# Sixteen merge-gate tiles computed as eight pairs of seven block products

## The reference

```python
h = rmsnorm(x, norm_mix_pre)
parts = split(h @ w_in, SPLIT_SIZES)          # ... last part: N_BRANCHES * D_MODEL gate logits
o_a = nsa_mixer(...)    # compressed, selected and sliding-window attention, 8 heads
o_b = gla_mixer(...)    # chunked gated linear attention, 4 heads
o_c = moba_mixer(...)   # causal attention over blocks, 8 heads of 64
merged = sum(sigmoid(gate_b) * (o_b @ w_branch_b) for the three branches)
x = x + rmsnorm(merged @ w_out, norm_mix_post)
x = x + rmsnorm(swiglu_ffn(rmsnorm(x, norm_ffn_pre)), norm_ffn_post)
```

## Time and profile before

| | us |
|---|---|
| median of 3 runs | 911.66 (911.61 to 911.70) |
| profiled execution, its own time | 911.39 |
| its span, first to last instruction | 909.7 |
| TensorE busy | 902.2 (99%) |
| VectorE busy | 632.3 (70%) |
| ScalarE busy | 494.6 (54%) |
| GpSimd busy | 176.1 (19%) |

### The profile page before, as it was taken

The page is one execution under the profiler, slowest core; times in us unless marked ns, Lnnn a source line. Parts: engine busy times, 40 slices in busy tenths (PEclk is TensorE's granted clock), DMA queues, the critical chain, the costliest instruction groups (busy, mean ns, idle before and its releaser), DMA issues.

```text
span 909.7 us, 14373 instructions
## 1 busy us (share of the span) xinstructions
PE 902.2 (99%) x5236; PEld 795.3 (87%) x5236; DVE 632.3 (70%) x1173; ACT 494.6 (54%) x928; POOL 176.1 (19%) x192
## 2 busy tenths in 40 slices
PE   9999999999999999999999999999999999999997
PEld 8888888888888888888888888989999999988886
DVE  5998656372555555656657748867888888779776
ACT  6744245343556665767664436345555655556562
POOL 3000254334133333435410001100001000000000
PEclk9999999999999999999999999999999999999999
DMA  9323626222323233274326943477777862334662
GB/s 346 127 74 89 200 93 214 88 93 93 101 85 96 91 101 103 84 266 127 122 91 253 329 149 116 151 154 229 188 245 204 227 173 101 108 159 161 210 205 96
DMA packets 43154, 139.62 MB, mean 153 GB/s; under 512 B 4884, under 2 KB 7508, under 8 KB 42332
## 3 DMA queue, kind: packets, MB, share of 16 engines
q1 hardware_dynamic: 37260, 116.16, 36.9%
q0 software_dynamic: 4992, 18.88, 9.0%
q10 hardware_dynamic: 832, 3.67, 1.4%
HBM read 124.83 MB, written 32.54 MB: 173 GB/s over the span
## 4 chain that ended last, share of the span: by engine, by line
PE 96%; DVE 2%; DMA 1%; ACT 1%; issue 0%; SPq 0%; DVEq 0%; ACTq 0%
PE bank L2237 27%; PE bank L2239 27%; PE bank L2238 27%; PE bank L833 3%; PE bank L825 2%; PE bank L850 2%; PE bank L848 2%; PE bank L824 2%; PE bank L2302 1%; PE bank L2256 1%; DMA xT<-x_features 1%; DVE pcs L685 1%; PE bank L2436 0%; PE bank L2492 0%; PE bank L2352 0%; PE bank L2423 0%
## 5 line engine op out<-in xcount | busy, mean ns | idle before, releaser
L1137 ACT ACTIVATE w_hi<-w_raw 128x1024 fp32r<-128x1024 f32 (+1 forms) x84 | 88.4, 1054 | 124.5 <-PE bank L2239 121.0
L2237 PE MATMUL bank<-h_hi,w_lo 128*128 128x512 f32 x352 | 140.5, 399 | 0.0
L2238 PE MATMUL bank<-h_lo,w_hi 128*128 128x512 f32 x352 | 137.5, 391 | 0.0
L2239 PE MATMUL bank<-h_hi,w_hi 128*128 128x512 f32 x352 | 137.4, 390 | 0.0
L1547 DVE TENSOR_TENSOR w_lo<-w_raw,w_hi 128x1024 fp32r<-128x1024 f32 (+2 forms) x63 | 77.0, 1223 | 40.5 <-ACT w_hi L1137 40.2
L712 DVE CUSTOM_DVE_ANT_0 sc<-bank,fullb 128x512 f32<-128x512 f32 (+1 forms) x96 | 47.0, 490 | 77.8 <-PE bank L825 76.0
L609 ACT ACTIVATE sc<-sc,ast 128x512 f32<-128x512 f32 (+1 forms) x96 | 53.8, 561 | 72.8 <-DVE ast L712 72.7
L1051 POOL TENSOR_TENSOR sc<-sc,ast 128x512 f32<-128x512 f32 (+1 forms) x96 | 66.3, 723 | 130.6 <-DVE ast L734 97.7
L2238 PE MATMUL bank<-tx_lo,op_hi 128*128 128x256 f32 x288 | 81.5, 283 | 0.0
L2239 PE MATMUL bank<-tx_hi,op_hi 128*128 128x256 f32 x288 | 81.5, 283 | 0.0
L2237 PE MATMUL bank<-tx_hi,op_lo 128*128 128x256 f32 x288 | 81.5, 283 | 0.0
(11 more groups left out here) (375 smaller groups left out, 2410.7 us busy)
## 6 DMA issues: line engine op xcount, KB each, us to landing
w_raw<-wpack SPq DMA_DIRECT2D x126, 512.0 KB, 3.7
down_sums<-wpack POOLq DMA_DIRECT2D x18, 768.0 KB, 7.0
dn_right<-down_sums SPq DMA_DIRECT2D x12, 768.0 KB, 4.2
dn_right<-wpack SPq DMA_DIRECT2D x9, 768.0 KB, 4.3
gate_logits<-gl_out SPq DMA_DIRECT2D x24, 256.0 KB, 2.2
gl_in<-gate_logits SPq DMA_DIRECT2D x24, 256.0 KB, 5.5
down_sums<-down_sums POOLq DMA_DIRECT2D x6, 768.0 KB, 5.9
near_bias<-near_bias ACTq DMA_DIRECT2D x1, 2880.0 KB, 13.5
```

The costliest lines, as they stand in the source:

```text
L1137: sa.activation(split_weights(c)[0][:, 0:n], raw[:, s, 0:n], ACT.Copy).then_inc(w_hi, 1)
L2237: mm(out, ll, rh, start=start, stop=False, skip_group_check=True)
L2238: mm(out, lh, rl, start=False, stop=False, skip_group_check=True)
L2239: return mm(out, lh, rh, start=False, stop=stop, skip_group_check=True)
```

## The change

Eight gate tiles stay as they are (units 0 to 31). The other sixteen are taken in pairs: two tiles are a 256 x 512 result, with a model dimension of 1024, and the pair is computed as a 2 x 2 block product with seven instead of eight block products (Winograd's form, the same as in the FFN). Each block product is 4 steps of `three` over 256 tokens. A pair takes eight units, with 4, 3, 4, 3, 4, 3, 4, 3 steps in them.

- **Weights.** The blocks b11, b12, b21, b22 are packed in the weight array; the sums t1 to t4 are made in DRAM by GpSimd with 16 copying and adding transfers of 1 MiB, fourteen in the straight stage and two in units 2 and 6 of the attention. A weight piece is now 128 x 512, and there are seven per pair, with splits and fetches at units set by a table.
- **Sums of h.** VectorE forms s1, s2, s4 and s3 of the halves of h in units 6 to 28 and 35, ScalarE their highs in units 13, 17, 23 and 34.
- **Results.** A pair uses two banks. ScalarE copies four intermediate results (256 columns each) and VectorE joins three, all at the head of a unit, for a product that ended in the unit before. Five buffers in SBUF hold the results: three for the left tile in turn, two for the right one. SP stores both tiles in the first two units of the next pair.
- **Room.** The sums and buffers lie where `cks` and `cv` were. So SP stores all MoBA keys and values to DRAM before the attention (2 MiB each), and loads keys, swapped keys and values per head into rings of two.

The diff, cut to what the text speaks of:

```diff
+G_PLAIN = 8
+G_PAIRS = (N_GATES - G_PLAIN) // 2
+GATE_OPS = (("b11", "a11"), ("t1", "s1"), ("t2", "s2"), ("b22", "s4"), ("t3", "s3"), ("b21", "a12"), ("t4", "a22"))
+STEP_FROM = (0, 4, 7, 11, 14, 18, 21, 25, 28)
...
+    at = {C_GATE + k: UNITS_PER_GATE * (k - 2) + 5 for k in range(2, G_PLAIN)}
...
+        at[C_PAIRED + o] = U_PAIRED + UNITS_PER_PAIR * q + (1, 3, 4, 5, 6, 7, 8)[i]
...
+EARLY_SUMS = {5 + 2 * n: divmod(n, 8) for n in range(14)}
+GATE_SUMS_AT = {2: (1, 6), 6: (1, 7)}
...
 # attention_act, at the head of unit u
+                if r == 1 and 0 <= q < G_PAIRS:
...
+                    gate_product(sa, len(GATE_OPS) * q)
+                    sa.activation(gl_left(q)[:, 0:256], pair_bank(q, 0), ACT.Copy).then_inc(gl_copied, 1)
+                elif r == 3 and 0 <= q < G_PAIRS:
...
+                    gate_product(sa, len(GATE_OPS) * q + 1)
+                    sa.activation(gl_right(q)[:, 256:512], pair_bank(q, 1), ACT.Copy).then_inc(gl_copied, 1)
...
 # attention_act, at the end of unit u
+                if u in (13, 17, 23):
...
+                    sa.activation(hs_hi[name][:, :, :], hs[name][:, :, :], ACT.Copy).then_inc(tx_hi, 1)
...
+                for c in HIGH_AT.get(u, ()):
+                    hi(c)
 # attention_dve: sums of h, then at the head of unit u the joins
+                if u == 6:
+                    ve.wait_ge(xT_in[2], 64)
+                    h_whole(h21, first, late)
+                elif u == 8:
+                    h_whole(h_other, second, late)
...
+                if r == 5 and 0 <= q < G_PAIRS:
+                    gate_product(ve, len(GATE_OPS) * q + 3)
+                    ve.wait_ge(gl_copied, G_PLAIN + GATE_COPIES * q + 3)
+                    ve.tensor_tensor(gl_right(q)[:, 0:256], pair_bank(q, 3), gl_right(q)[:, 0:256],
+                                     ALU.subtract).then_inc(joined_out, 1)
...
-                if u % 4 == 2 and 0 <= u // 4 - 1 < N_GATES + 2:
-                    lo(C_GATE + u // 4 + 1)
+                h_sums(u)
+                for c in LOW_AT.get(u, ()):
+                    lo(c)
 # attention_pe
+                elif u < len(UNITS):
+                    q, r = divmod(u - U_PAIRED, UNITS_PER_PAIR)
+                    for step in range(STEP_FROM[r], STEP_FROM[r + 1]):
+                        gate_step(te, three, q, *divmod(step, 4))
...
+        def gate_step(te, three, q, i, k):
...
+                elif i == 1:
+                    te.wait_ge(gl_copied, G_PLAIN + GATE_COPIES * q)
+                elif i < 5:
+                    te.wait_ge(gl_copied, G_PLAIN + GATE_COPIES * q + i - 1)
+                else:
+                    te.wait_ge(joined_out, 3 * q + i - 4)
...
 # SP
+            for t in range(NT):
+                sp.wait_ge(tm_free[t], TM_USE["cv"] + 1)
+            sp.dma_start(cv_dram.rearrange("n p d -> p n d"), cv[:, :, :, :].rearrange("p n t d -> p n (t d)").bitcast(F32)
+                         ).then_inc(xT_in[2], 16)
             single_out(sp, slot_of("ck", 3))
             single_out(sp, slot_of("ck", 2))
-            swap(ckx[:, 0, :], cks[:, 0, :], ck_swap[0])
+            sp.dma_start(ck_dram.rearrange("n p d -> p n d"), cks[:, :, :].bitcast(F32)).then_inc(xT_in[2], 16)
...
                     if n >= 8:
-                        swap(ckx[:, n % 2, :], cks[:, n - 6, :], ck_swap[n % 2])
+                        moba_keys(n + 2)
...
+                n = LAST_OF.get(u - PV_LAG - 1)
+                if n is not None and 8 <= n < N_HEADS - 2:
+                    sp.wait_ge(pv_done, u - PV_LAG)
+                    moba_values(n + 2)
...
+                for c in FETCH_AT.get(u, ()):
+                    if c == C_BR + 3:
+                        sp.wait_ge(gl_stored[1], 16 * (N_GATES // 2))
+                    fetch(c)
 # GpSimd, straight stage, after the low of chunk c + 2
+                if c in EARLY_SUMS:
+                    pool.wait_ge(w_hi, c + 1)
+                    gate_sums(*EARLY_SUMS[c])
```

More of the change, by code:

```diff
@@ L149, with split_at, by_unit, packed_row @@
 assert UNITS_PER_GATE * N_GATES == len(UNITS) and UNITS_PER_GATE == 4
+U_PAIRED, UNITS_PER_PAIR = UNITS_PER_GATE * G_PLAIN, 2 * UNITS_PER_GATE
+STEP_FROM = (0, 4, 7, 11, 14, 18, 21, 25, 28)
+def split_at():
+    at = {C_GATE + k: UNITS_PER_GATE * (k - 2) + 5 for k in range(2, G_PLAIN)}
+    for o in range(4):
+        at[C_PAIRED + o] = U_PAIRED - 3 + (0, 1, 3, 3)[o]
+    for o in range(4, N_GATE_OPS):
+        q, i = divmod(o - 4, len(GATE_OPS))
+        at[C_PAIRED + o] = U_PAIRED + UNITS_PER_PAIR * q + (1, 3, 4, 5, 6, 7, 8)[i]
+    at[C_BR], at[C_BR + 1] = len(UNITS) - 2, len(UNITS)
+    at[C_BR + 2], at[C_BR + 3] = len(UNITS) + 5, len(UNITS) + 9
+    return at
+def by_unit(table):
+    units = {}
+    for c in sorted(table):
+        units.setdefault(table[c], []).append(c)
+    return units
+SPLIT_AT = split_at()
+HIGH_AT = by_unit(SPLIT_AT)
+LOW_AT = by_unit({c: u + 1 for c, u in SPLIT_AT.items()})
+FETCH_AT = by_unit({c: max(len(UNITS) + 2 if c == C_BR + 3 else 3, SPLIT_AT.get(c - RAW_SLOTS, 0) + 1 + (c < C_PAIRED + RAW_SLOTS)) for c in range(C_GATE + RAW_SLOTS, C_BR + RAW_SLOTS)})
+EARLY_SUMS = {5 + 2 * n: divmod(n, 8) for n in range(14)}
+GATE_SUMS_AT = {2: (1, 6), 6: (1, 7)}
+def packed_row(c):
+    return c if c < C_PAIRED else c - PACKED_LESS
 def operand(p, name):
@@ L408, in program, with gate_product, pair_bank, gl_left @@
         block = ctx.enter_context(nc.Block())
+        def gate_product(eng, o):
+            eng.wait_ge(w_used, C_PAIRED + o + 1)
+        def pair_bank(q, i):
+            return bank[6 + (q + (i in (1, 3, 5))) % 2][:, 0:256]
+        def gl_left(q):
+            return gl_first if q == 0 else gl_out if q % 2 else gl_later
+        def gl_right(q):
+            return raw[:, (C_BR + 3) % RAW_SLOTS, 512:CHUNK] if q % 2 else gl_even[:, :]
+        def right_of(name, k):
+            if name in hs:
+                return hs_hi[name][:, k, :], hs_low[name][:, k, :]
+            row = 4 * (name in ("a12", "a22")) + k
+            mine = slice(256, 512) if name in ("s3", "a22") else slice(0, 256)
+            return hh[:, row, mine], hl[:, row, mine]
         def landed(eng, slot, turn):
@@ L806, in branch_part @@
                 last.then_inc(p_full if part == 0 else w_used, 1)
+        def gate_step(te, three, q, i, k):
+            o = len(GATE_OPS) * q + i
+            c = C_PAIRED + o
+            right = GATE_OPS[i][1]
+            if k == 0:
+                te.wait_ge(w_hi, c + 1)
+                lo_split(te, c)
+                if i == 0 and q == 0:
+                    te.wait_ge(gl_copied, G_PLAIN - 1)
+                elif i == 0:
+                    te.wait_ge(joined_out, 3 * q)
+                elif i == 1:
+                    te.wait_ge(gl_copied, G_PLAIN + GATE_COPIES * q)
+                elif i < 5:
+                    te.wait_ge(gl_copied, G_PLAIN + GATE_COPIES * q + i - 1)
+                else:
+                    te.wait_ge(joined_out, 3 * q + i - 4)
+                if q == 0 and 1 <= i <= 4:
+                    te.wait_ge(tx_lo, i)
+            xh, xl = right_of(right, k)
+            high, low = split_weights(c)
+            cols = slice(P * k, P * k + P)
+            last = three(pair_bank(q, i), high[:, cols], low[:, cols], xh, xl,
+                         i in (0, 1, 5) and k == 0, i in (3, 5, 6) and k == 3)
+            if k == 3:
+                last.then_inc(w_used, 1)
         def attention_pe(te, mm, three):
@@ L894, in swap, with moba_keys, moba_values @@
                 sp.dma_start(dst[0:64].bitcast(F32), src[64:128].bitcast(F32)).then_inc(done, 16)
+            def moba_keys(n, swapped=True, own=True):
+                if swapped:
+                    for half in range(2):
+                        rows, other = slice(64 * half, 64 * half + 64), slice(64 - 64 * half, 128 - 64 * half)
+                        sp.dma_start(ckx[rows, n % 2, :].bitcast(F32), ck_dram[n - 8, other, :]).then_inc(ck_swap[n % 2], 16)
+                if own:
+                    sp.dma_start(ckr[:, n % 2, :].bitcast(F32), ck_dram[n - 8, :, :]).then_inc(ck_swap[n % 2], 16)
+            def moba_values(n):
+                sp.dma_start(cvr[:, n % 2, :, :].rearrange("p t d -> p (t d)").bitcast(F32), cv_dram[n - 8, :, :]
+                             ).then_inc(xT_in[n % 2], 16)
             def near_bias(n):
```

242 lines of the change are left out of this document (199 added, 43 removed).

## The result

| | before | after |
|---|---|---|
| median | 911.66 us (5 runs, 911.61 to 912.24) | 916.55 us (5 runs, 915.07 to 917.44) |
| profiled span | 909.7 us | 914.8 us |

What follows compares the result with a forecast made beforehand. TensorE's own work, busy 99% of the span, was taken as the bound. Terms -6.7 + 0.5 + 0.5 + 1.0 = -4.7 us took the profiled 911.39 to 906.7, with 0.27 for the median 907.0; range 902 to 912.5.

Steps and rivals of the forecast that it cites:

- TensorE, -6.7 us: Gate parts of paired tiles: 5.14 us per pass against 5.56, over 16 passes 6.7 us saved; bounds 3.9 to 9.4.
- Rival 4: Gate matmuls: weight load binds, starts over 131 ns; at 150 ns a pair loses 1.5 us, so 924; chance 0.02.
- ScalarE and VectorE within the pairs: Pair passes: neither engine is over capacity, order counts; 0.5 us booked for lost units, bounds 0 to 2.5.
- Rival 1: MoBA passes: ScalarE takes over, its 2.63 us waits per pass all stay, so 920; chance 0.11.
- Sums of h: First 32 units: VectorE's twelve operations of 1.226 us, 14.7 us, fit in 26 us of idle time; booked at nothing.
- The sixth unit: VectorE waits for MoBA keys and values to reach DRAM before the first h sum; 0.5 us, bounds 0 and 2.6.
- The burst: Start of MoBA: queued loads of 5.77 MB make keys for unit 80 late; 1.0 us, bounds 0 and 3.0.
- GpSimd's sums in DRAM: GpSimd issues 16 DRAM sums of 1 MiB, about 9.3 us each; booked at nothing, up to 1.5 us.
- the gain is eaten by stalls: Sixth unit, burst and lags at their bounds (2.6 + 3.0 + 2.5) cancel 6.7 and more: 911 to 913; chance 0.12.

Runs made afterwards that it cites:

- e3: Changed kernel with GLA's 2 MiB load-back in eight pieces at units 73 to 87 and the logit loads at units 89 to 95; 911.11 us.
- e9: e4 with ScalarE's high of `h21` right behind its first right copy at the head of unit 35, the low left in place; 906.93 us.
- e1: Changed kernel with VectorE's eleven operations on h of units 6 to 28 one unit later, ScalarE's highs at units 15, 19, 23; 914.04 us.
- e11: Changed kernel with VectorE's eleven operations on h one unit later, ScalarE's highs left at units 13, 17 and 23; 913.99 us.
- e4: Changed kernel with the edits of e1 and e3, plus the store of a finished gate tile ahead of its unit's fetch; 908.10 us.
- e2: Changed kernel with the twelve h operations and four highs cut to two columns per row, TensorE reading unsummed h; 912.40 us.
- e7: Changed kernel with the 2 MiB load-back issued on ScalarE's queue at the same unit; 915.21 us.
- e8: e4 with ScalarE's high of `h21` at the end of unit 35 and its low at unit 36; 909.32 us.
- e12: Changed kernel with only ScalarE's highs moved, to units 15, 19 and 23, VectorE's h operations left in place; 916.94 us.
- e5: Changed kernel with only the h operations of units 18 and 26 moved, to 19 and 27; 918.43 us.
- e6: Changed kernel with the six h operations of units 8, 12, 16, 20, 24 and 28 one unit later; 915.69 us.

## Why the prediction was wrong

**TensorE, -6.7 us: right.** 42 starts of 120 ns, 5.05 us against the 5.14 forecast. Ten passes gained 4.36 us, 0.44 each; sixteen would give 7.0. Rival 4, the weight load, did not come: the starts lie well below its limit (11.1 us over 84 starts is 132 ns; the prediction has 131).

**ScalarE and VectorE within the pairs, 0.5 us: about right.** The passes from unit 36 to 75 are 8.62 to 8.93 us without a wait of note. In MoBA two passes (76 and 84) stay at 9.28 to 9.3 in e3 and e9, 0.65 us above their neighbours; some 0.2 of it is a wait for a probability low, the rest stays open (VectorE, forecast at 15.0 of 17.4 us, is busy 18.47 of 20 us there, from 436 to 456 us). Rival 1, ScalarE taking over, did not come: undisturbed, it still idles 0.50 + 0.20 + 0.55 + 0.52 = 1.77 us in a pass of 9.3, against the earlier trace rows; I had forecast 0.9.

```profile
435.26 0.62 ACT L737 ACTIVATE sc<-sc,ast 128x384 f32<-128x384 f32 x1 [0.50 <-DVE ast L902]
437.82 0.51 ACT L737 ACTIVATE sc<-sc,ast 128x256 f32<-128x256 f32 x1 [0.20 <-DVE ast L902]
439.65 0.40 ACT L737 ACTIVATE sc<-sc,ast 128x128 f32<-128x128 f32 x1 [0.55 <-DVE ast L902]
441.73 0.72 ACT L737 ACTIVATE sc<-sc,ast 128x512 f32<-128x512 f32 x1 [0.52 <-DVE ast L902]
```

**Sums of h, booked at nothing: the first step that failed, 3.6 us.** The prediction counted idle time (26 us) against work (14.7 us) and let a unit run over into a next one that "has no second large operation". The count was not at fault: it took a MoBA stretch, but from 236 to 312 us, where the sums stand, the kernel before leaves VectorE idle for 32.3 of 76 us, which is more. Three other things were wrong. The 1.226 us came from a row in which VectorE had SBUF to itself, and half of the operations were put right where GpSimd starts its scaling: 1.95 to 2.02 us. The next step of TensorE's chain, the maximum, stands directly behind, so idle time elsewhere in the pass is no cover. And the delay does not stay on VectorE: by way of the exponential it reaches ScalarE's weight high and comes back as VectorE's wait for it (1.14 us). e1 shows the place as the cause, since the same work one unit later costs nothing up to unit 32, and e11 shows VectorE's part of it. The rest is the pass of unit 32, 1.25 us longer than before and 1.64 longer than in e9, and there it is ScalarE: the high of `h21`, which I had booked with the sums, stands ahead of the copy that TensorE waits for, behind another copy that waited 2.63 us for a store. With the high behind the copy the pass falls by 0.9 us (9.67 to 8.74, e4 to e9), of which the next pass takes back 0.4; the 0.4 us of the store ahead of the fetch (10.10 to 9.67, e1 to e4) are within the scatter of this pass.

That slowing was to be had from the Trainium skill before the fact ("GPSIMD Engine Reference", section "Key points"): GpSimd shares its SBUF interfaces with VectorE and contends with VectorE instructions that have two SBUF inputs. The trace agrees, 2.02 against 1.21 us and 3.74 against 2.76. The page gives no price, and by itself the rule would have misled too: e1 has the scaling slow and loses nothing.

**The sixth unit, 0.5 us: right in size.** VectorE waits 0.4 us for the dump of the keys, and unit 12 starts 0.45 us later. With the sum in unit 7 it is gone (e1), and with VectorE's wait but a short operation behind it too (e2); so it takes the wait and the full sum in that place together.

**The burst, 1.0 us with a bound of 3.0: the second step that failed, 5.7 us.** The mechanism was the one named, with place and releaser; the size was not. The prediction had 5.77 MB at 340 GB/s from unit 72, the keys 18.2 us later. They came 22.3 us after it (398.42 to 420.76), 4.1 us later than that. Its count was right: SyncE's list from 398.42 to the keys adds up to 5.5 MiB. But some 7.1 MB moved in that time (317 GB/s over 22.3 us), 1.3 more than counted; by the same list they must be what was still under way at unit 72, such as a fetch issued just before it, and transfers issued behind the keys (values and three weight pieces, 1 MiB, from 411.40 to 415.19 us). At 340 GB/s 1.3 MB is 3.9 us. The remaining 0.2 us is the slow start, 171 GB/s in the stretch from 400 to 402 us, less what the later 365 to 393 GB/s gave back: SyncE issued the load-back only at 404.62, 3.8 us into unit 73, behind a store (402.74) and a fetch (404.19), which by the code wait for a join and for a weight low. TensorE itself came 18.1 us after unit 72 instead of 17.4, so the wait is 4.2 us. To it come 1.6 us at the lower clock, for which the sum had no term at all. That the term would be nothing with another queue is not borne out, as far as e7 goes: with the load-back on a queue of its own 2.8 us of wait stay, and the keys take as long to land, though still behind the logits. Nor do loads in one queue land strictly in the order of their issue: in the changed kernel a weight piece issued at 408.39 landed 10.6 us later, and the two swapped key loads issued behind it, from 409.61 on, took 8.3 and 8.4 us and were there before it.

**GpSimd's sums in DRAM, at nothing: about right.** Twelve take 8.7 us each and four 6.4, against the 9.3 taken. The attention starts 0.38 us later than before in the changed kernel, and from 0.30 earlier to 0.72 later in the experiments (2.15 in the profiled execution of e4). **The rivals.** That the gain is eaten by stalls had 0.12, with a price of 911 to 913, and is what happened; it went past its bounds because both stalls did. That e9 comes out at 906.93, where the prediction had 907.0, is no excuse: it is the time of another order of the same work.

## What to carry to other kernels

Idle time counts only between the two steps that it separates: before adding work to an engine that is 70% busy, look at what stands directly behind it in that queue, and what the neighbours do at that moment. A bound for a burst should start from when the queue really issues, and a wait of TensorE of the length seen here should be booked with the lower clock behind it. When a change brings less than its arithmetic, put the lengths of its stages side by side: here one table showed the gain whole and two losses of another origin, both curable by moving work.

## What the runs showed of the hardware

- A VectorE operation on two SBUF operands of 128 x 1024 takes 1.21 us alone and up to 2.02 beside GpSimd's scaling, whose four operations go from 2.76 to 3.74 us (4.02 at unit 16 of e1).
- TensorE's granted clock fell to 0.50 (1.2 GHz) in nine waits of 2.0 to 5.7 us: shortly behind the end of those of 2.0, 2.2, 2.3, 2.8 and 4.2 us (e2, e8, e1, e7, after), and while TensorE still waited in those of 4.0, 4.3, 5.5 and 5.7 us (e12, e5, e6, e11). It stayed at 1.00 behind one of 1.06 us (unit 35 of the changed kernel). In seven of the nine it was back at 1.00 within 5 us of the end of the wait, and the fall cost 1.6 to 1.8 us beside the wait. In e5 and e12 it took almost 6 us, and the pass from unit 80 was 11.31 and 11.42 us, 2.6 and 2.8 above e3's; why is open.
- Behind the burst the keys for unit 80 took 8.3 to 10.5 us from issue to landing, whichever queue the load-back stood in (10.1 in e7); without it 4.9 (e3) and 4.1 (e9).
- The same burst delayed the same keys by 2.0 to 5.7 us in different executions, and the kernels that have it spread more: 911.2 to 915.9 us in ten executions of e1, 910.3 to 912.2 in ten of e3, which has not, and 910.9 to 912.7 for the kernel before beside them.
